# A Trainium2 kernel of two fused transformer blocks: the normed activations, and every tile above them, move 192 bytes up in SBUF

## What is computed

```python
# first_block, two layers; every "@" is a product with a large fp32 weight
x = x + 0.5 * swiglu(rmsnorm(x, g[0]), ffn_w_in, ffn_w_out)     # 1024 -> 2*2816 -> 1024
x = x + mixer(rmsnorm(x, g[1]))    # layer 0: a gated linear recurrence; layer 1: latent attention, 16 heads
x = x + 0.5 * swiglu(rmsnorm(x, g[2]), ...)
x = x + sigmoid(rmsnorm(x, g[3]) @ ple_w_gate) * (p @ ple_w_in)
# after layer 0: keys and values of the latent attention from x; at the end: final rmsnorm
# second_block, two layers
h = rmsnorm(x, g_pre) * (1 + scale) + shift       # scale, shift, gate from a small vector c
x = x + gate * rmsnorm(hybrid_mixer(h, w_in, w_out), g_post)   # two kinds of attention, 8 + 8 heads
```

## The kernel before

| tile | what it is | byte offset | mod 256 |
|---|---|---|---|
| `w_raw`, `w_hi`, `w_lo` | weight chunks; slots are 8192 apart | 16512, 32896, 65664 | 128 |
| `X`, `sq`, `rs`, `ones`, `const` | residual, squares, 1/rms, constants | 98432 to 117376 | 128 |
| `ckh`, `ckl` | split latent of the keys | 128704, 130752 | 192 |
| `xh`, `xl` | split normed activations, 1024 bytes a row block | 139840, 148032 | 64 |
| `hh`, `hl` | split hidden of a feed-forward | 156224, 178752 | 64 |
| `oh`, `ol`; `hg_oh`, `hg_ol` | split mixer outputs | 156224, 172608; 164416, 180800 | 64 |
| `cqh`, `cql`; `pth`, `ptl` | split query latent; split embedding | 217664, 221760; 203328, 205376 | 64 |
| `mod_raw`, `mod_acc` | the vector path that makes scale, shift, gate | 217664, 220736 | 64 |

## Time and profile before

### The profile page before, as it was taken

The page is one execution under the profiler, slowest core; times in us unless marked ns, Lnnn a source line. Parts: engine busy times, 40 slices in busy tenths (PEclk is TensorE's granted clock), DMA queues, the critical chain, the costliest instruction groups (busy, mean ns, idle before and its releaser), DMA issues.

```text
span 1597.3 us, 31108 instructions
## 1 busy us (share of the span) xinstructions
PE 1519.2 (95%) x12299; PEld 1460.1 (91%) x12299; DVE 1105.5 (69%) x1648; ACT 779.5 (49%) x1259; POOL 202.8 (13%) x239
## 2 busy tenths in 40 slices
PE   6999998989999989999999999999987998989998
PEld 6999998989999989999989799999977976889767
DVE  5886559966886586876677745976578448394583
ACT  5554375355544356544352634544364338254481
POOL 1111015601421010111010001101023000120000
PEclk9999999999999999999999999999998999999999
DMA  7787744325776645766645254876555503085010
GB/s 225 223 273 244 232 133 133 111 75 169 248 245 215 226 124 177 256 222 200 223 116 149 80 159 152 276 233 212 180 158 159 162 27 106 1 239 174 14 54 27
DMA packets 219309, 264.86 MB, mean 166 GB/s; under 512 B 22253, under 2 KB 197325, under 8 KB 219213
## 3 DMA queue, kind: packets, MB, share of 16 engines
q1 hardware_dynamic: 209136, 234.58, 47.0%
q0 software_dynamic: 8960, 27.37, 5.2%
q10 hardware_dynamic: 1117, 1.57, 0.3%
HBM read 262.44 MB, written 1.05 MB: 165 GB/s over the span
## 4 chain that ended last, share of the span: by engine, by line
PE 79%; DVE 11%; ACT 5%; DMA 2%; issue 1%; POOL 0%; SPq 0%; DVEq 0%; ACTq 0%
PE bank L1049 23%; PE bank L1051 23%; PE bank L1050 23%; DVE w_lo L1717 4%; PE bank L1617 2%; PE bank L1456 1%; PE bank L1650 1%; DVE rs L1729 1%; ACT w_hi L688 1%; DVE hg_s L1917 1%; PE bank L1470 1%; PE bank L1468 1%; PE bank L1063 1%; ACT sC L928 1%; DMA w_raw<-in_ffn_w_in 1%
## 5 line engine op out<-in xcount | busy, mean ns | idle before, releaser
L688 ACT ACTIVATE w_hi<-w_raw 128x1024 fp32r<-128x1024 f32 x452 | 454.3, 1039 | 466.0 <-PE bank L1051 312.4
L1049 PE MATMUL bank<-xh,w_lo 128*128 128x256 f32 x2312 | 652.5, 282 | 24.5 <-DVE xl L2176 14.2
L1717 DVE TENSOR_TENSOR w_lo<-w_raw,w_hi 128x1024 fp32r<-128x1024 f32 x452 | 549.4, 1251 | 148.5 <-ACT w_hi L688 147.4
L1050 PE MATMUL bank<-xl,w_hi 128*128 128x256 f32 x2312 | 647.8, 280 | 0.0
L1051 PE MATMUL bank<-xh,w_hi 128*128 128x256 f32 x2312 | 647.7, 280 | 0.0
L1049 PEld LDWEIGHTS bank<-xh,w_lo 128*128 128x128 f32 x2312 | 438.1, 189 | 28.9 <-DVE xl L2176 14.9
L1050 PEld LDWEIGHTS bank<-xl,w_hi 128*128 128x128 f32 x2312 | 437.4, 189 | 1.1 <-issue 0.7
L1051 PEld LDWEIGHTS bank<-xh,w_hi 128*128 128x128 f32 x2312 | 436.9, 189 | 0.3
L1049 PE MATMUL bank<-hh,w_lo 128*128 (+1 forms) x704 | 194.7, 277 | 0.0
L1050 PE MATMUL bank<-hl,w_hi 128*128 (+1 forms) x704 | 194.3, 276 | 0.0
L1051 PE MATMUL bank<-hh,w_hi 128*128 (+1 forms) x704 | 194.3, 276 | 0.0
(11 more groups left out here) (367 smaller groups left out, 2213.4 us busy)
## 6 DMA issues: line engine op xcount, KB each, us to landing
w_raw<-in_ffn_w_in SPq DMA_DIRECT2D x176, 512.0 KB, 4.7
w_raw<-in_ffn_w_out SPq DMA_DIRECT2D x88, 512.0 KB, 4.4
w_raw<-in_w_in SPq DMA_DIRECT2D x52, 512.0 KB, 4.5
mod_raw<-in_w_ada POOLq DMA_DIRECT2D x128, 192.0 KB, 4.4
w_raw<-in_a_w_in SPq DMA_DIRECT2D x32, 512.0 KB, 4.5
w_raw<-in_ple_w_gate SPq DMA_DIRECT2D x16, 512.0 KB, 4.5
w_raw<-in_b_w_out SPq DMA_DIRECT2D x16, 512.0 KB, 3.6
w_raw<-in_w_out SPq DMA_DIRECT2D x16, 512.0 KB, 3.5
```

The source lines that it names most:

```text
L688: A(w_hi[:, c % NSLOT, cols], w_raw[:, c % NRAW, cols], ACT.Copy).then_inc(*did(hi_ready))
L1049: mm(out, lhs[1], rhs[0], start=start, stop=False, skip_group_check=skip)
L1050: mm(out, lhs[0], rhs[1], start=False, stop=False, skip_group_check=skip)
L1717: V.tensor_tensor(w_lo[:, c % NSLOT, cols], w_raw[:, c % NRAW, cols], f32(w_hi[:, c % NSLOT, cols]), ALU.subtract).then_inc(*did(lo_ready))
```

## The change

One line is added. Behind `ptok` the running offset is raised by 192 bytes before `xh` is placed.

```diff
     ptok = fixed("ptok", [P, 2, TB, T])
+    base[0] += 192
     xh = fixed("xh", [P, KD, T], F32R)
     xl = fixed("xl", [P, KD, T], F32R)
     region = base[0]
```

## The result

The changed kernel takes 1629.88 us (median of 4 runs, 1628.66 to 1635.21) against 1603.89 us for the kernel before on the same chip (4 runs, 1594.97 to 1607.21). The ratio is 1.0177, 95% interval 1.013 to 1.0225: slower, where the prediction said 1579 us and faster, and outside its range of 1558 to 1611 us. The profiled execution has a span of 1626.8 us, 29.5 us more than before, at the same mean clock (0.982; before 0.983).

A forecast was written before the change was run, and what follows sets the result against it. It took TensorE to bound the kernel, through matmul count times the distance between starts. From the profiled 1599.1 us it took off 20.2 for 95 slow chunks going fast, other terms 0, giving 1579 us, range 1558 to 1611.

The forecast's parts named there:

- What bounds the kernel: Whole kernel: TensorE sets the time, as number of matmuls times the distance between starts; the change acts only through that distance.
- The two paces: Split matmul streams: fast 113.3 ns and slow 117.8 ns a matmul, 4.43 ns or 0.213 us a chunk apart.
- two read streams that meet: Inside TensorE: matmul and weight load beside it meet in the same part of memory, and both lose some ns.
- Part (1): Split products going from 64 to 128 bytes apart: 95 slow chunks all go fast, -20.2 us.
- four outcomes: Split products at the new distance: all fast 0.42, deeper (below the fast pace) 0.10, as now 0.28, slow 0.20.
- The bound from the other side: Split products: if the new distance makes all 121 fast chunks slow, +25.8 us.
- Rival (b): Split products: 128 bytes is the bad distance if places repeat every 128 bytes; hidden streams slow first, 1625 us; chance 0.20.
- Rival (a): Split products: address is no lever, order of starts inside TensorE picks the pace; 1599 us, 1592 to 1610; chance 0.28.
- (2): Products with `ckh`/`ckl`: distance stays 64, both paces stay; 0, at most 0.4 us.
- (3): The fp32 products of scores, transposes and values: 0, with 1 us either way.
- (4): ACT, DVE, POOL and DMA reading and writing the moved tiles: 0, with 1 us either way.
- The test that I had named: Hidden stream above 48.96 us for nine chunks and above 276 ns would show 128 bytes is the bad distance.

The follow-up runs named there:

- the small program: Separate kernel running only split matmuls at chosen operand distances, not a changed kernel; with weights at rest 128, 113.3 ns at distance 112, 120.0 at 0.

## Why the prediction was wrong

**What bounds the kernel: right.** Time is the number of matmuls times the distance between two starts; the change acted through that alone. The two paces and their sizes were borne out, and so was that a stream keeps its pace, with the addition that a gap can draw it anew. The reading as two read streams that meet fits, in that the pace follows the places of both operands, in stretches in which no other engine works; what happens inside TensorE no trace shows.

**Part (1): the step that failed.** "If all go fast: 95 x 0.213 = -20.2 us. That is the term I take" had no row behind its sign. The prediction named four outcomes, had no row at the new distance, and took all fast as the likeliest (0.42, against 0.20 for slow) because the slow pace looked like a collision that a larger distance would clear. Distance 128 does not clear it; it puts nearly every stream at 118.7 or 120.0 ns. The term measured +36.3 us of longer steps in place of -20.2: some 121 fast chunks lose 0.255 us each (5.695 - 5.440), 30.9 us; the 95 chunks at 117.8 ns lose 0.042 each, 4 us; the rest is in streams at 120.0.

**The bound from the other side** (+25.8 us, all at the slow pace) was too small, because it took the slow pace of before, 117.8, for the worst there is. Nearest rows bound a pace only if the new place is like the old ones; here there were levels outside both (118.7, 120.0). The span grew by 29.5 us and not by 36.3, since 6.8 us went elsewhere, 5.0 of them idle time of TensorE. That the total came out near the bound of 25.8 is luck: the bound had the wrong pace and no idle time given back.

**Rival (b)** gave the place and about the size of what happened (hidden streams above 48.96 us and 276 ns, 1625 against 1629.9), for a wrong reason. Its period of 128 bytes is refuted: distance 0 gives 120.0 and distance 128 mostly 118.7, and in the small program 112 gives 113.3 and 240 gives 117.0 to 117.3. The argument used against it, that fp32 products of two tiles at distance 0 run at 111.7 ns, was no evidence: those have 64 moving columns of plain fp32, and the load sets their distance, so they can't show what a 256-column fp32r stream loses.

**Rival (a)**, the address is no lever, is refuted by the paces of 118.7 and 120.0 ns, which no stream of before had and which come and go with one offset. (The 1.3% of the kernel with `+= 128` alone would not do it: both its paces are those of before.) The rule that spoke for it fares no better. The Trainium skill (TensorE: Matmul & The Clock Gate, Part 2: What happens when you issue a matmul) has the weight load take nothing from a running matmul's reads; by the place of one operand alone these runs show 6.7 ns a matmul between distances 112 and 0 (113.3 and 120.0), and more at 116 (121.8), so by the measurement the two are not independent here. The prediction's own term needed the rule to be false as well, and it was given no weight against that term.

**Parts (2), (3), (4): right.** `ckh` and `ckl` kept their paces (113.3 and 117.8), the fp32 products of `hg_f` stand 112 ns apart in the median in both kernels, the other engines' busy times agree to 1.5 us, and the DMA share in the loops is no higher than in the earlier trace rows.

**The test that I had named** was decisive in one view: "the hidden stream above 48.96 us for nine chunks", and it is 51.27.

## What to carry to other kernels

Where TensorE bounds the time and every matmul has a weight load of its own, read the distance between matmul starts stretch by stretch. Here the same code at two paces meant that something as small as an offset, or what stood right before the stream, was deciding. Before moving a tile, measure the pace at the new place in a small program that runs only that product; a term that no row shows can have either sign, and its far end can lie outside the values seen. An offset must be judged as a pair, moving operand against weights, and exactly, not by a rule such as "further apart".

## What the runs showed of the hardware

- For a 128 x 128 weight tile and 256 moving columns of fp32r at full clock, the pace depended on the distance of the two operands modulo 256 bytes: 113.3 ns (at best) at 64, 112 and 192, 118.5 to 120.0 at 128, 120.0 at 0, 80 and 96, 121.8 at 116. No stream settled under 113.3, and 4 bytes beside 112 and 192 it was lost.
- At 64 and 192 two paces exist, 113.3 and 117.8. A stream kept the one it had over hundreds of matmuls, until a gap; behind a gap of 0.15 us and one of 0.8 us it was the other. Behind a small matmul put ahead of them, 7 of 8 loops went from the slow to the fast one.
- The first 12 steps of a stream behind the fp32 matmul took 121 to 133 ns each on average in the small program, at every distance.
- Left open: what in the start picks the pace; why weights at 144 with activations at 0 lose the fast pace at distance 112; how the two paces were shared out in the executions that were only timed; and what the two operands do to each other inside TensorE. A size other than 256 columns, or another type, was not tried.
